# One matmul order for feature-major products: a depth tile's three passes go to the slot's two output tiles in turn

## The reference, cut to what matters

```
def swiglu(u, w13, w2):
    a, b = jnp.split(u @ w13, 2, axis=-1)
    return (jax.nn.silu(a) * b) @ w2

def project(u, w_in, b_in, conv_w, conv_b):
    p = u @ w_in + b_in
    ...

def hybrid_mixer(x, w_in, conv_w, ...):
    proj = jnp.einsum("bld,dp->blp", x, w_in)
    qkv, z, a, b, uv, gate_dn, gate_sgu = jnp.split(proj, offsets, axis=-1)
    qkv = jax.nn.silu(causal_depthwise_conv(qkv, conv_w)).astype(f32)
    ...
```

## Time and profile before

| | |
|---|---|
| time, median of 3 runs | 2736.75 us (2736.74 to 2738.9) |
| span of the profiled execution | 2732.5 us |
| time of the median run less that span | 4.25 us |
| TensorE busy | 2583.3 us (95%), 14430 matmuls and as many weight loads |
| VectorE, ScalarE, GpSimd busy | 1166.0, 757.4, 1322.8 us |
| mean granted TensorE clock | 0.973 of full speed |

### The profile page before, as it was taken

How to read it: one execution, slowest core, us unless ns; L and a number is a source line. 1 busy time by engine, 2 the same in 40 slices (tenths; PEclk the granted TensorE clock), 3 DMA queues, 4 the chain that set the end, 5 groups by cost and what they waited for, 6 DMA issues and landing times. The chain is left out here.

```text
span 2732.5 us, 36022 instructions
## 1 busy us (share of the span) xinstructions
PE 2583.3 (95%) x14430; PEld 2204.8 (81%) x14430; DVE 1166.0 (43%) x1704; ACT 757.4 (28%) x1216; POOL 1322.8 (48%) x425
## 2 busy tenths in 40 slices
PE   7999999998999999998999998999989999969997
PEld 5888888887899788876888886878887898857775
DVE  5112101167764553026111215364435144359997
ACT  5111001135120432105100104334431012127774
POOL 1343455441563047673777775555427776610000
PEclk8999999999999999999999998999999999979999
DMA  7443121123321022232223224120012322539994
GB/s 296 185 185 144 65 77 61 62 97 118 111 77 64 1 96 77 77 142 78 92 79 113 87 84 192 64 76 1 1 63 93 124 93 93 185 130 395 374 373 172
DMA packets 52850, 334.60 MB, mean 122 GB/s; under 512 B 6660, under 2 KB 7684, under 8 KB 20016
## 3 DMA queue, kind: packets, MB, share of 16 engines
q1 hardware_dynamic: 51136, 327.02, 32.2%
q0 software_dynamic: 1584, 5.78, 0.5%
HBM read 314.41 MB, written 22.07 MB: 123 GB/s over the span
## 5 line engine op out<-in xcount | busy, mean ns | idle before, releaser
L186 POOL TENSOR_TENSOR whi<-raw,one_col 128x2048 fp32r<-128x2048 f32 (+2 forms) x155 | 515.8, 3328 | 857.9 <-PE bank L206 767.7
L189 POOL TENSOR_TENSOR wlo<-raw,whi 128x2048 fp32r<-128x2048 f32 (+2 forms) x155 | 676.7, 4366 | 12.1
L204 PE MATMUL bank<-uh_a,whi 128*128 128x512 f32 (+1 forms) x704 | 239.1, 340 | 0.0
L205 PE MATMUL bank<-ul_a,whi 128*128 128x512 f32 (+1 forms) x704 | 237.8, 338 | 0.0
L206 PE MATMUL bank<-uh_a,wlo 128*128 128x512 f32 (+1 forms) x704 | 237.5, 337 | 0.0
L3938 DVE TENSOR_TENSOR moe_wl<-moe_raw,moe_wh 128x2048 fp32r<-128x2048 f32 x84 | 189.4, 2282 | 7.2 <-DMA xs_scratch<-moe_tok,moe_dest 5.4
L3874 ACT ACTIVATE moe_wh<-moe_raw 128x2048 fp32r<-128x2048 f32 x84 | 159.8, 1912 | 25.6 <-PE bank L3849 19.7
L204 PEld LDWEIGHTS bank<-uh_a,whi 128*128 128x128 f32 x704 | 134.3, 191 | 18.3 <-issue 4.1
L204 PE MATMUL bank<-uh_b,whi 128*128 128x512 f32 x352 | 138.9, 394 | 8.1 <-DVE ul_b L1066 7.1
L206 PEld LDWEIGHTS bank<-uh_a,wlo 128*128 128x128 f32 x704 | 134.2, 191 | 14.3
L205 PEld LDWEIGHTS bank<-ul_a,whi 128*128 128x128 f32 x704 | 134.3, 191 | 14.0
(11 more groups left out here) (633 smaller groups left out, 6366.0 us busy)
## 6 DMA issues: line engine op xcount, KB each, us to landing
moe_raw<-moe_w_dram SPq DMA_DIRECT2D x84, 1024.0 KB, 7.4
cond_ring<-w_ada_dram SPq DMA_DIRECT2D x27, 1024.0 KB, 7.0
raw<-gu_a_dram SPq DMA_DIRECT2D x22, 1024.0 KB, 6.9
raw<-gu_b_dram SPq DMA_DIRECT2D x22, 1024.0 KB, 4.9
raw<-wqkv_dram SPq DMA_DIRECT2D x12, 1024.0 KB, 4.8
raw<-dn_a_dram SPq DMA_DIRECT2D x16, 704.0 KB, 4.1
raw<-dn_b_dram SPq DMA_DIRECT2D x16, 704.0 KB, 4.1
n_ada<-w_ada_dram SPq DMA_DIRECT2D x9, 1024.0 KB, 21.6
```

What stands on the lines that cost most here:

```text
L186: e.nc.gpsimd.tensor_tensor(e.whi[p][:, 0:f], e.raw[p][:, 0:f], e.one_col[:, 0:1].to_broadcast([P, f]), ALU.mult).then_inc(e.w_hi, 1)
L189: e.nc.gpsimd.tensor_tensor(e.wlo[p][:, 0:f], e.raw[p][:, 0:f], e.whi[p][:, 0:f].bitcast(F32), ALU.subtract).then_inc(e.w_split, 1)
L204: e.nc.tensor.matmul(out, wh, xh, start=first, stop=False)
L205: e.nc.tensor.matmul(out, wh, xl, start=False, stop=False)
```

## The change

The two orders become one. k is the outer loop everywhere; within a depth tile the three passes are the next loop, and the output tiles the inner one. So matmul after matmul goes to the other bank, where before the bank changed after three matmuls (with `ready`) or once, after 24. The number of matmuls and their operands are the same. `between` is called ahead of depth tile kt/2 in place of ahead of output tile 1. `half` is raised by the last matmul that writes output tile 0, which is now the one before the slot's last. The context products behind, and the products with one output tile, keep their order.

```
-    order = [(n, k) for k in range(kt) for n in range(ntile)] if ready is not None else \
-        [(n, k) for n in range(ntile) for k in range(kt)]
-    for n, k in order:
-        if between is not None and (n, k) == (ntile - 1, 0):
+    for k in range(kt):
+        if between is not None and k == kt // 2:
             between()
-        if ready is not None and n == 0:
+        if ready is not None:
             ready(k)
-        at = (n * kt + k) * P
-        done = three_pass(e, e.bank[2 * p + n][:, :], wh[:, at:at + P], wl[:, at:at + P],
-                          xh[:, k, 0:T], xl[:, k, 0:T], k == 0, k == kt - 1)
-        if half is not None and (n, k) == (0, kt - 1):
-            done.then_inc(half, 1)
+        for a, b, first, last in ((wh, xh, k == 0, False), (wh, xl, False, False), (wl, xh, False, k == kt - 1)):
+            for n in range(ntile):
+                at = (n * kt + k) * P
+                done = e.nc.tensor.matmul(e.bank[2 * p + n][:, :], a[:, at:at + P], b[:, k, 0:T], start=first, stop=last)
+                if half is not None and last and n == 0:
+                    done.then_inc(half, 1)
```

## The result

| | before | after |
|---|---|---|
| time, median of 20 runs each | 2737.04 us (2732.65 to 2742.58) | 2740.73 us (2735.98 to 2747.04) |
| ratio to before, 95% interval | | 1.0014 (1.0008 to 1.0021) |
| span of the profiled execution | 2732.5 us | 2740.4 us |
| mean granted TensorE clock | 0.973 | 0.971 |

The change makes the kernel 3.7 us slower, 0.14%. Where a run lay far out (5349.03 us once in experiment 2, 3055.43 us once in experiment 6, a few of the kernel before), it counts in the median given and not in the ratio.

The account below looks back on a forecast made before the run. TensorE, busy 95% of the span, was taken as the bound. Pace 0, waits 0 and half signal +1.7 us on the 2732.5 us span, plus 4.25 us to the median run, gave 2738.4 us, range 2734 to 2743 us.

Parts of the forecast that it names:

- The pace: 5232 two-output-tile matmuls, 226.6 ns apart: changing the bank at every matmul was to cost or gain 0.
- The rounding limit of 6.8 us: Most the pace could move the time either way, 5232 matmuls at 1.3 ns, given the trace's 0.01 us rounding.
- Rivals 1 and 2: Pace gains 12.8 ns a matmul, 2670 us (chance 0.05); pace loses 6.0 ns a matmul, 2768 us (chance 0.06).
- Rival 3: TensorE's clock falls in the slots, 1.7 us per low stretch, 2919 us if in each of 107; chance 0.03.
- Waits in the slot: `ready`, `between` and the slot ends keep their places in the two-output-tile slots: 0.
- The half signal: Last `wqkv2` slot: `half_done` comes 6.58 us later, mostly covered; taps start 1.69 us late, counted in full.
- Rival 4: The half signal is hidden after all, or the low stretch falls better: 2736.8 us, no change; chance 0.06.
- The clock: Low-clock stretch behind `wqkv2`: no difference from 1.69 us more idle time, with 1.7 us either way kept as bounds.
- The sum: Whole kernel: 0 for pace, 0 for waits, +1.7 us for the half signal, 2738.4 us, 0.06% slower, read as same.
- The range: Whole kernel: 0 to +3.4 us, widened by 2.2 us run scatter on both sides, rounded to 2734 to 2743 us.

Follow-up runs that it names:

- experiment 2: Kernel before, all its orders kept, with the half signal raised behind matmul 47 of the slot in place of 24: 2742.11 us, ratio 1.0015.
- experiment 6: Kernel before with decay row operations behind first taps and subtractions in ScalarE's exponential: 2729.63 us; same on changed kernel: 2732.50 us; exponential alone on kernel before: 2735.65 us.
- experiment 1: Changed kernel, but the one slot with the half signal keeps the old order: 2737.89 us, ratio 1.0000.
- experiment 3: Kernel before with the half signal raised behind matmul 36 in place of 24: 2738.06 us, ratio 1.0001.
- both of 4: Kernel before with the half signal behind matmul 47, plus filling matmuls in TensorE's idle time behind the last `wqkv2` slot: 36 gave 2740.54 us, 18 gave 2736.57 us.

## Why the prediction was right, and where its size was off

**The pace.** Right, and for the reason given: the first slot of `w_dn` before already changed banks every third matmul and took the same 10.88 us. The rounding limit of 6.8 us either way was far too wide; the traces leave 0.1 us, and experiment 1 puts 106 slots at a ratio of 1.0000. Rivals 1 and 2 fall with it. Rival 3 falls as well: the clock stays at 1.00 inside the slots of `w_dn`, and 106 slots in the new order cost nothing in experiment 1.

**Waits in the slot.** Right: the slot ends, `between` and `ready` cost nothing, by the same experiment.

**The half signal.** The mechanism was right, each step of it: the copy right behind the last but one matmul (it ends at 1840.83 + 0.39 = 1841.22 us, the copy starts at 1841.32, 0.10 us behind it where 0.04 were forecast), the two copies in one piece, six taps in one piece, `keep`, transposes and GpSimd's mask late in turn. (The mask is 9.07 us behind the last matmul, 7.02 us before: 2.05 us later, as the `keep` that it waits for stands behind transposes at the low clock.) 1.69 us were forecast for the taps and 1.75 us measured; the 0.06 us are those of the copy. The forecast also said why only a part of the 6.58 us counts, and experiment 3 shows the cover: 4.1 us of delay cost nothing. Rival 4, that it would be hidden, falls by experiment 2.

**The clock.** This is the term that was mis-sized. The forecast took "no difference" from a longer idle time, with 1.7 us as the bound on either side. All four profiles with the late signal and no fill have a low stretch of 6.8 us, and all six with the signal on time (or at 36) and no fill one of 3.4 us. It belongs to the idle time, as filling it shows. Where the forecast had 0, the longer stretch measures 0.8 to 1.0 us by the first preparation, in four of four pairs, and inside the bound. Another 1.2 us come by `wz2` in three of the four pairs, as the delta rule has 6.8 us in place of 3.4 us at 1.2 GHz there; in the fourth it goes the other way. That these belong to the signal is not shown.

**The sum.** 1.75 + 0.9 = 2.65 us are shown, against 3.7 us measured between the medians and 3.8 us by the ratio (2 to 6 us by the interval). With the delta rule's 1.2 us, as three pairs have it, the sum would be 3.85 us. The forecast of 2738.4 us lies 2.3 us under the measured 2740.73 us. 0.3 us of that are the kernel before, whose median of 20 is 2737.04 us, and 2.0 us the size. (The 4.25 us added to the span hold some 2.4 us by which the profiled execution lay under the median: in all later runs the time is 1.8 to 1.9 us above the span.) The range held it because it was made wide for the scatter of the runs, not because the clock's term was right.

**The 3.5 us at the start of `wqkv2`** are no part of the change. The kernel before has runs as high as 2742.58 us and as low as 2732.65 us, and whether VectorE is held there is probably one thing that parts them. Of the seven kernels with the subtractions ahead of the taps, five were held for 3.6 us in their profiled execution: after, 1, 3 and both of 4. Each of these executions (2742.26, 2740.60, 2740.47, 2746.50 and 2738.72 us) is above its kernel's median, and that of experiment 2, which wasn't held, is below it (2739.81 against 2742.11 us). As three of the five have the old order, it is not the new order that holds VectorE. That the changed kernel is held more often than the kernel before is not excluded by one profile each; experiments 1 and 2, which give the whole difference to the half signal, leave little room for it.

## What to carry to other kernels

Before an order of matmuls is changed for their pace, look for a slot that already runs in the new order: a `ready` slot and a plain one side by side gave the answer. Then list every semaphore that the old order raised in the middle: each is a consumer's early start, and what it is worth is read from when that consumer was free, not from how far the signal moves. A wait that TensorE gets in front of a chain of short matmuls is to be looked at twice, once as the wait and once for the stretch at 1.2 GHz that may follow it. Here the first was 1.75 us and the second 0.8 to 1.0 us. One profile of each kernel is not enough for such sizes, as the low stretches of a later stage fall differently from one execution to the next.

## What the runs showed of the hardware that was not expected

- An idle time of 2.8 us of TensorE was followed by 3.4 us at 1.2 GHz in each of six profiles, one of 4.56 us by 6.8 us in each of four. Filled to 0.54 us or less, there was none in each of four.
- The idle time alone does not set the stretch. One of 2.61 us near the end of the delta rule was followed by 3.4 us at 1.2 GHz in eight of the fourteen profiles, by 6.8 us in five and by none in one. One of 3.6 to 3.7 us in `wz2` was followed by none in the kernel before (3.64 us) and by 3.4 us in the kernel after (3.68 us).
- A float32 matmul of 128 columns in the source ran as two instructions: 36 came as 72 (8.20 us), 18 as 36 (4.18 us). The transposes of the same shape came as one each (8 as 8).
- Operations of VectorE on 8 partitions by 128 elements that take 0.27 us took 3.6 to 4.6 us when they started within 0.1 us behind an operation of GpSimd on other tiles, and ended with it. In the kernel before all four ended 0.12 us ahead of GpSimd's operation and none was held.
